# Three of the eleven down-projection units computed with seven block products in place of eight

## What is computed

```
def swiglu(x, w_gate, w_up, w_down):
    return (jax.nn.silu(x @ w_gate) * (x @ w_up)) @ w_down

h = h + 0.5 * swiglu(rms_norm(h, ln_ffn1[layer]), ffn1_w_gate[layer],
                     ffn1_w_up[layer], ffn1_w_down[layer])
```

## Time and profile before

| | us |
|---|---|
| median of 3 runs | 918.43 |
| the profiled execution, its own time | 919.42 |
| its span, first to last instruction | 917.6 |
| TensorE busy in the span | 905.8 (99%) |
| VectorE busy | 574.0 (63%) |
| ScalarE busy | 471.6 (51%) |
| share of the chain that ended last: TensorE / VectorE / DMA | 91% / 4% / 2% |

### The profile page before, as it was taken

One profiled execution on the slowest core, in us unless ns is written; L12 is line 12 of the kernel. 1 busy time (PEld: TensorE's weight loads), 2 busy tenths in 40 slices (PEclk: granted clock), 3 DMA queues, 4 the chain that ended last, 5 costly groups with the idle time before them and its releaser, 6 DMA issues.

```text
span 917.6 us, 11621 instructions
## 1 busy us (share of the span) xinstructions
PE 905.8 (99%) x4195; PEld 745.5 (81%) x4195; DVE 574.0 (63%) x724; ACT 471.6 (51%) x635; POOL 90.7 (10%) x170
## 2 busy tenths in 40 slices
PE   8999999999999999999999999999999999999997
PEld 7888888888888888888888888888876788888885
DVE  5656663574787766665467566644588776656542
ACT  6554443565685654444346445433478664444431
POOL 1100005623311100000002000000030000000000
PEclk9999999999999999999999999999999999999999
DMA  9898778558733888876557888874563388887611
GB/s 306 258 296 240 240 243 243 209 180 289 234 98 93 263 266 261 246 261 230 178 162 231 251 249 249 301 243 171 196 230 110 121 279 272 263 252 285 228 71 46
DMA packets 169758, 202.86 MB, mean 221 GB/s; under 512 B 15160, under 2 KB 139136, under 8 KB 169712
## 3 DMA queue, kind: packets, MB, share of 16 engines
q1 hardware_dynamic: 168752, 201.37, 67.5%
q0 software_dynamic: 512, 0.36, 0.4%
q10 hardware_dynamic: 448, 0.53, 0.2%
HBM read 184.39 MB, written 17.83 MB: 220 GB/s over the span
## 4 chain that ended last, share of the span: by engine, by line
PE 91%; DVE 4%; DMA 2%; issue 1%; ACT 1%; SPq 1%; POOL 0%; POOLq 0%; DVEq 0%; ACTq 0%
PE bank L535 58%; PE bank L574 18%; PE bank L580 9%; PE bank L596 2%; PE bank L764 1%; PE bank L639 1%; DVE w_lo L1767 1%; PE bank L795 1%; DMA raw<-in_ffn_w_up 1%; DMA x_bounce<-silu 0%; PE bank L817 0%; PE bank L741 0%; SPq L1055 0%; ACT junk L1399 0%; DVE hT_lo L1767 0%
## 5 line engine op out<-in xcount | busy, mean ns | idle before, releaser
L1767 DVE TENSOR_TENSOR w_lo<-raw,w_hi 128x2048 fp32r<-128x2048 f32 x149 | 340.2, 2292 | 185.5 <-ACT w_hi L1380 185.1
L1380 ACT ACTIVATE w_hi<-raw 128x2048 fp32r<-128x2048 f32 x154 | 294.4, 1916 | 194.3 <-PE bank L580 97.6
L535 PE MATMUL bank<-w_hi,xT_hi 128*128 128x512 f32 x816 | 318.8, 391 | 0.2 <-DVE w_lo L1774 0.2
L535 PE MATMUL bank<-w_lo,xT_hi 128*128 128x512 f32 x816 | 317.6, 389 | 0.0
L535 PE MATMUL bank<-w_hi,xT_lo 128*128 128x512 f32 x816 | 307.9, 389 | 0.0
L535 PEld LDWEIGHTS bank<-w_hi,xT_hi 128*128 128x128 f32 x816 | 153.2, 188 | 33.1 <-DVE w_lo L1774 0.6
L535 PEld LDWEIGHTS bank<-w_hi,xT_lo 128*128 128x128 f32 x816 | 153.2, 188 | 31.9
L535 PEld LDWEIGHTS bank<-w_lo,xT_hi 128*128 128x128 f32 x816 | 153.2, 188 | 31.3
L574 PE MATMUL bank<-w_hi,hT_hi 128*128 128x512 f32 x348 | 135.6, 390 | 0.0
L574 PE MATMUL bank<-w_lo,hT_hi 128*128 128x512 f32 x348 | 135.4, 389 | 0.0
L580 PE MATMUL bank<-w_hi,hT_lo 128*128 128x512 f32 x348 | 107.1, 389 | 0.0
(11 more groups left out here) (182 smaller groups left out, 599.7 us busy)
## 6 DMA issues: line engine op xcount, KB each, us to landing
raw<-in_ffn_w_down SPq DMA_DIRECT2D x88, 512.0 KB, 5.1
raw<-in_ffn_w_gate SPq DMA_DIRECT2D x86, 512.0 KB, 5.9
raw<-in_ffn_w_up SPq DMA_DIRECT2D x86, 512.0 KB, 7.0
raw<-in_a_w_qkv SPq DMA_DIRECT2D x24, 512.0 KB, 5.6
h_bounce<-silu SPq DMA_DIRECT2D x40, 256.0 KB, 7.0
xn<-h_bounce SPq DMA_DIRECT2D x160, 64.0 KB, 3.0
xn<-x_bounce SPq DMA_DIRECT2D x64, 64.0 KB, 2.0
raw<-in_a_w_o SPq DMA_DIRECT2D x8, 512.0 KB, 5.3
```

The lines of the kernel that those rows point to most:

```text
L535: mm = nc.tensor.matmul(bank[b][:, :], xs[:, kt, own(pos)], ws[:, slot(u), cols], start=(kt == 0 and i == 0), stop=(kt == KT - 1 and i == 2))
L1380: nc.scalar.activation(w_parts(u)[0], raw[:, slot(u), :], ACT.Copy).then_inc(s_hi, 1)
L1767: nc.vector.tensor_tensor(lo, raw[:, slot(u), :], hi.bitcast(F32), ALU.subtract).then_inc(s_lo, 1)
```

## The change

Three of the eleven down units (positions 2, 4 and 6 of the order, `SEVEN`) are computed with seven block products (21 matmuls in place of 24), by sums and differences of blocks:

- Four sums of h tiles for each such unit (`h_sum`, 128 x 128 each, and a copy `a1_copied` of the first rows' tiles), made in each loop turn of the gate and up part on VectorE, ahead of `mul(1, 0)` and the split of unit 4g+6. They are split too (`h_sums_high` on ScalarE, `h_sum_low` on VectorE) and held where `vec` was.
- Four sums of weight tiles: one in place in `raw` before the unit is split (`t_first`), three of 512 columns beside it (`t_sums`), split by `t_high` (ScalarE, 1536 columns) and `t_low` (VectorE). There is room for the three of one unit alone (over `xT_hi`, `xT_lo`); those of the next unit wait until TensorE has read them (`s_t_used`).
- Banks 4 to 7 gather four of the products over the three units; `seven_added` adds them into x with eight VectorE instructions after the last split.
- The order of the down part is two units of first rows, two of second rows, then unit by unit up to the seventh; the tiles of h are taken in the order `DN_ORDER`. The bias vectors are loaded later, since their place holds the sums until then.

The diff, cut to what computes and orders (new semaphores and views left out):

```
+DN_ORDER = [1, 3, 0, 5, 2, 6, 4, 7, 8, 9, 10]
+SEVEN = [2, 4, 6]
+N_SEVEN = len(SEVEN)
+SEVEN_END = SEVEN[-1] + 1
...
+        with nc.sbuf_tensor("t_raw", [P, KT * SEQ], F32) as t_raw:
+            pass
         xT_lo = sb("xT_lo", [P, KT, SEQ], F32R)
...
-        vec = sb("vec", [P, VEC_RING, D])
+        with nc.sbuf_tensor("vec", [P, VEC_RING, D], F32) as vec:
+            pass
+        h_sums = sb("h_sums", [P, VEC_RING, 2, BANK], F32R)
...
+            def three(b, lhs, rhs, start=False, stop=False):
+                (l_hi, l_lo), (r_hi, r_lo) = lhs, rhs
+                nc.tensor.matmul(bank[b][:, :], l_hi, r_hi, start=start, stop=False)
+                nc.tensor.matmul(bank[b][:, :], l_hi, r_lo, start=False, stop=False)
+                return nc.tensor.matmul(bank[b][:, :], l_lo, r_hi, start=False, stop=stop)
+            def seven(f, u, n):
...
+                T2, T4, T3 = range(3)
+                begin, end = n == 0, n == N_SEVEN - 1
+                pe.wait_ge(s_h_sums_lo, seven_no(f, n))
+                pe.wait_ge(s_t_lo, seven_no(f, n))
+                for b in (4, 5, 6, 7) if begin else ():
+                    take(b)
+                three(6, s_tile(3), t_tile(T3), begin, end)
+                three(5, s_tile(2), t_tile(T2), begin, end)
+                three(acc(1, 0), a_tile(1, 1), t_tile(T4)).then_inc(s_t_used, 1)
+                unit_ready(u)
+                three(7, s_tile(1), b_tile(0, 1), begin, end)
+                three(4, a_tile(0, 0), b_tile(0, 0), begin, end)
+                three(acc(0, 0), a_tile(0, 1), b_tile(1, 0))
+                three(acc(0, 1), s_tile(4), b_tile(1, 1)).then_inc(s_used, 1)
...
-                        rows_pass(u0 + GU_UNITS + i, 2 * i, FT, pos, hT_hi, hT_lo, ("down", f))
+                        rows_pass(u0 + GU_UNITS + i, 2 * DN_ORDER[i], FT, pos, hT_hi, hT_lo, ("down", f),
+                                  first=(i == 0))
                 pe.wait_ge(s_hT_lo[0], block_no(f, H_BLOCKS - 1))
-                down((0, 1, 2), 0)
+                down((0, 1), 0)
                 pe.wait_ge(s_hT_lo[1], block_no(f, H_BLOCKS - 2))
-                down((0, 1, 2), 1)
-                down((3, 4, 5, 6), 0)
-                down((3, 4, 5, 6), 1)
+                down((0, 1), 1)
+                for i in range(2, SEVEN_END):
+                    if i in SEVEN:
+                        seven(f, u0 + GU_UNITS + i, SEVEN.index(i))
+                    else:
+                        down((i,), 0)
+                        down((i,), 1)
...
+                        if i - UNITS_HELD in SEVEN:
+                            sp.wait_ge(s_t_sums, seven_no(f, SEVEN.index(i - UNITS_HELD)))
+                        load(u, [(dst[:, k, :], view[:, 2 * DN_ORDER[i] + k, :]) for k in range(2)])
...
-                for name in vectors:
-                    vector(name)
...
-                down(*range(8, DN_UNITS))
+                down(8, 9)
+                if "b_b_q" in vectors:
+                    vector("b_b_q", u0)
+                down(10)
+                for name in vectors:
+                    if name != "b_b_q":
+                        vector(name, u0)
...
-                if n == 2:
-                    sp.wait_ge(s_lamd, 1)
+                sp.wait_ge(s_used, u0 + GU_UNITS + SEVEN[n] + 1)
                 sp.dma_start(vec[:, n, :], src.to_broadcast([P, D])).then_inc(s_vec[n], 16)
...
+            def t_high(f, n):
+                act.wait_ge(s_t_sums, seven_no(f, n))
+                nc.scalar.activation(t_hi[:, 0:3 * BANK], t_raw[:, 0:3 * BANK], ACT.Copy).then_inc(s_t_hi, 1)
+            def h_sums_high(f, turn):
+                act.wait_ge(s_h_sums, turn + seven_no(f, 0))
+                nc.scalar.activation(h_sums[:, bass.ds(turn, 1), 0, :], vec[:, bass.ds(turn, 1), BANK:D],
+                                     ACT.Copy).then_inc(s_h_sums_hi, 1)
...
                     silu_gate(1, 0, g, turn)
+                    if turn is not None:
+                        h_sums_high(f, turn)
                     split(u0 + 4 * g + 6, turn)
...
-                split(u0 + 24)
+                split_with_t1(u0 + 24, f, 0)
+                silu_gate(1, 0, 5)
+                t_high(f, 0)
                 split(u0 + 25)
-                silu_gate(1, 0, 5)
-                split(u0 + 26)
+                split_with_t1(u0 + 26, f, 1)
                 h_hi(1, 4)
-                for i in range(27, 30):
-                    split(u0 + i)
+                split(u0 + 27)
+                t_high(f, 1)
+                split_with_t1(u0 + 28, f, 2)
                 h_last_hi(0)
                 h_last_hi(1)
+                split(u0 + 29)
+                t_high(f, 2)
                 for i in range(30, 33):
                     split(u0 + i)
+                act.wait_ge(s_used, u0 + GU_UNITS + SEVEN_END)
+                nc.scalar.activation(p1_copy, bank[4][:, :], ACT.Copy).then_inc(s_read[4], 1)
...
+            def t_first(f, u, n):
+                dve.wait_ge(s_raw[slot(u)], 32 * (u // UNITS_HELD + 1))
+                nc.vector.tensor_tensor(raw_tile(u, 0, 1), raw_tile(u, 0, 1), raw_tile(u, 0, 0),
+                                        ALU.add).then_inc(s_t1, 1)
+            def t_sums(f, u, n):
+                if n == 0:
+                    dve.wait_ge(s_used, u - SEVEN[0])
+                else:
+                    dve.wait_ge(s_t_used, seven_no(f, n) - 1)
+                dve.wait_ge(s_t1, seven_no(f, n))
+                t2, t4, t3 = [t_raw[:, BANK * i:BANK * (i + 1)] for i in range(3)]
+                link(nc.vector.tensor_tensor(t2, raw_tile(u, 0, 1), raw_tile(u, 1, 1), ALU.add))
+                nc.vector.tensor_tensor(t4, t2, raw_tile(u, 1, 0), ALU.add)
+                nc.vector.tensor_tensor(t3, t2, raw_tile(u, 0, 0), ALU.subtract).then_inc(s_t_sums, 1)
+            def t_low(f, n):
+                dve.wait_ge(s_t_hi, seven_no(f, n))
+                cols = slice(0, 3 * BANK)
+                nc.vector.tensor_tensor(t_lo[:, cols], t_raw[:, cols], t_hi[:, cols].bitcast(F32),
+                                        ALU.subtract).then_inc(s_t_lo, 1)
...
+                link(nc.vector.tensor_tensor(s_raw_tile(1), a_tile(1, 0), a_tile(1, 1), ALU.subtract))
+                link(nc.vector.tensor_tensor(s_raw_tile(2), a_tile(0, 0), s_raw_tile(1), ALU.subtract))
+                nc.vector.tensor_tensor(s_raw_tile(3), a_tile(1, 0), a_tile(0, 0), ALU.subtract)
+                nc.vector.tensor_tensor(s_raw_tile(4), a_tile(0, 1), s_raw_tile(2),
+                                        ALU.subtract).then_inc(s_h_sums, 1)
+            def a1_copied():
+                link(nc.vector.tensor_copy(a1_copy.rearrange("p (t q s) -> p t q s", t=2, q=4),
+                                           landed[0].rearrange("p (q t s) -> p t q s", q=4, t=4)[:, 0:2, :, :]))
...
+            def h_sum_low(f, turn):
+                dve.wait_ge(s_h_sums_hi, turn + seven_no(f, 0))
+                buf = bass.ds(turn, 1)
+                nc.vector.tensor_tensor(h_sums[:, buf, 1, :], vec[:, buf, BANK:D], h_sums[:, buf, 0, :].bitcast(F32),
+                                        ALU.subtract).then_inc(s_h_sums_lo, 1)
...
+                in_sbuf(dve, ("seven", f, 4))
+                nc.vector.tensor_tensor(p6_less, bank[5][:, :], p1_copy, ALU.subtract).then_inc(s_read[5], 1)
+                counted(into_x(0, 0, p1_copy, 0.5))
+                in_sbuf(dve, ("seven", f, 5))
+                nc.vector.tensor_tensor(p5_more, bank[7][:, :], p6_less, ALU.add).then_inc(s_read[7], 1)
+                counted(into_x(1, 0, p6_less, -0.5))
+                in_sbuf(dve, ("seven", f, 7))
+                counted(into_x(0, 1, p5_more, 0.5))
+                counted(into_x(1, 1, p5_more, 0.5))
+                dve.wait_ge(s_dve, t.last("dve"))
+                counted(into_x(1, 0, bank[6][:, :], -0.5))
+                ins = into_x(1, 1, bank[6][:, :], 0.5)
+                ins.then_inc(s_read[6], 1)
+                dve.wait_ge(s_dve, t.last("dve"))
+                in_sbuf(dve, ("seven", f, 6))
...
+                    if turn is not None:
+                        h_sum(f, turn)
                     if g == 0:
                         dve.wait_ge(s_rstd, rstd_count(name, 1))
                     mul(1, 0)
+                    if turn is not None:
+                        h_sum_low(f, turn)
...
                     mul(0, 0)
+                    if g < 4:
+                        a1_copied()
...
-                split(u0 + 24)
-                split(u0 + 25)
+                t_first(f, u0 + 24, 0)
                 h_last_turned(0)
                 dve.wait_ge(s_turned[1], block_no(f, H_BLOCKS - 1))
+                split(u0 + 24)
+                t_sums(f, u0 + 24, 0)
                 mul(1, 0, 5)
                 h_last_turned(1)
+                t_low(f, 0)
+                split(u0 + 25)
+                t_first(f, u0 + 26, 1)
                 split(u0 + 26)
                 h_lo(1, 4)
```

(11 more changed lines are left out.)

68 lines of the change are left out of this document (60 added, 8 removed).

## The result

The changed kernel takes 931.18 us (median of 4 runs, 930.35 to 931.89) against 919.0 us (4 runs, 918.35 to 919.94) before: ratio 1.0127, 95% interval 1.0115 to 1.0140. That is 12.2 us slower, outside the range forecast (911.5 to 929.5). The profiled execution took 930.35 us; its span is 928.5, 10.9 more than before.

The account below looks back on a forecast made before the run. TensorE, busy 99%, was taken to bound the kernel, so every wait put on it is paid. Removed matmuls -8.2, loop +7.4 and down part +5.6 gave +4.8 us: 923.2 us, range 911.5 to 929.5.

Parts of the forecast that it names:

- Removed, -8.2: Down units: 36 matmuls fewer at 0.2267 us each, all on the path, save 8.2 us.
- Loop, +7.4 forecast: Gate and up loop: sums delay ScalarE's copy and unit 4g+6's remainder; TensorE loses 0.62 us in each of 12 turns.
- late h at nothing: Loop: second-row h, sent some 3.4 us later, returns just before `h_lo` reads it; 0 us, up to 0.5 a turn.
- Down part, +5.6 forecast: Down part: second seven-product unit's weight sums come 1.29 us late, 1.4 with restart, in each of four feed-forwards.
- ruled it out: Down part, feed-forward 1: bank 2 is wanted at 422.6 and `mul` frees it at 421.3, so no wait.
- +4.8: Whole kernel: the sum -8.2 + 7.4 + 5.6 us, giving 923.2 against the median.
- rival 3: Loop: h returns later than `h_lo` wants it, 0.5 us more a turn, 6 in all: 929; chance 0.10 (or worse).
- The 7.1 us: Loop: time taken for h of the second rows to come back after it is sent.
- rival 1: Loop: sequencer steps hide behind short additions, TensorE waits about 0.1 a turn, 1.2 in all: 917.0; chance 0.19 with nearby.
- the rule: VectorE: next instruction starts when the pipe has emptied, semaphores cost nothing more; four additions take 1.16 us, time about 917.
- No wait at the first and third unit: Down part: first unit's sums ready before 428.03; third's end near 448.4, wanted at 449.8, 1.4 us of cover.
- `seven_added` covered: End of down part: eight VectorE additions end at 464.2, first rows at 465.5; 1.3 us of cover, priced at nothing.

Follow-up runs that it names:

- The removal alone: Kernel before with three matmuls left out in each of three down units (36 fewer), nothing added: 911.21 us.
- lighter loads: Changed kernel with half of each feed-forward weight load left out, except the first eight units of feed-forward 0: 924.6 us; same on the kernel before: 919.15.
- the doubled run: Changed kernel with the four h-sum additions of each loop turn made twice, ahead of `mul(1, 0)`: 948.1 us.

## Why the prediction was wrong

- **Removed, -8.2: right.** The removal alone gives 8.2, and with the added work well placed nothing of it is lost.
- **Loop, +7.4 forecast, +10.5 measured.** The quiet turn took 0.62, as forecast, and by the chain as written: from `h_lo` the four starts are 0.60, 0.43, 0.45 and 0.21 apart, against 0.60, 0.47, 0.47 and 0.21. That it fits to the hundredth is luck: the chain up to the end of the remainder was 0.09 shorter, and TensorE started 0.14 after it, where 0.05 was taken. The step that failed is the one that put late h at nothing: h "comes back just ahead of where `h_lo` of the next turn would read it, so I price it at nothing". For the blocks that the change sends later this held: in the second and third turns h was at most 0.04 late. But in the first loop turns of feed-forwards 1 and 3 `h_lo` reads the block of turn 0, which no sums stand ahead of and which the prediction didn't look at. It came 1.03 and 1.95 late, 3.0 us together, once the slack of 3.2 that had covered it was spent.
- **Down part, +5.6 forecast, +8.9 measured.** In feed-forwards 1 and 2 the second sums were late by the chain I wrote: 17.06 us after the start of the down part, forecast 16.99. The wait in full is 1.56, not 1.4: the chain ended 0.07 later, and TensorE starts 0.15 after the remainder, where 0.05 was taken. That is 0.6 in all. In feed-forwards 0 and 3 the block of h that stands ahead of `t_first` came back late, and the chain began later (ScalarE's copy of the third unit 1.48 and 0.71 us before TensorE's start in place of 2.44): 0.9 and 1.0 more. In feed-forward 3 `mul`, which frees bank 2, ended at 866.75, and TensorE wanted that bank 5.44 after its start, at 866.26: I take this for its wait at 866.85, 0.7 in full (the profile names no releaser; with lighter loads the wait is gone). I had ruled it out from feed-forward 1 alone.
- **Sum.** Late h is 3.0 + 1.9 + 0.7 = 5.6 of the 6.1 by which the profiled execution (+10.9) misses +4.8; lighter loads give 5.6 back between the profiled executions. This is rival 3, with its mechanism right and its place and size wrong. I gave it 0.10 and a price of 0.5 in every turn, having read a return that was in time as one that is always in time. The 7.1 us that I gave for h coming back is only the way out, up to SyncE's issue of the read. In the trace of before, the returns without cover were there to see (ScalarE's copy at 338.90, `h_lo` 0.46 idle at 774.44), and I read a feed-forward in which h was back with time to spare.
- **Cheap small steps, rival 1: half shown.** In this kernel's loop dependent additions are 0.43 to 0.45 apart, near the 0.47 taken; in the second set of the doubled run they are 0.32. What makes the difference was not tried. By the rule of the Trainium skill, "VectorE: DVE Perf Modes", "The DRAIN you can't avoid", four additions of 0.29 would take 1.16 us from first start to last end. The trace has 554.71 to 556.09, 1.38, so for the loop's own set the rows decide against it; for the second set, 594.14 to 595.28, it is 1.14, close to the rule. The prediction also gave the rule without its exception: the same page of the Trainium skill has a section, "Two Vector instructions with no wait between them", by which an instruction that nothing holds starts earlier, and the independent additions 0.20 apart with 0.28 of length agree.
- **No wait at the first and third unit, `seven_added` covered: right.** The eight additions of feed-forward 1 end at 469.28 and the residual begins at 471.03, 1.75 of cover (1.3 forecast).

## What to carry to other kernels

Work put ahead of an engine's critical step costs what the *waiting* engine loses: the same additions cost 11 us while ScalarE's copy of a unit stood behind them, and nothing once it stood ahead. Slack is cover for everything upstream, late transfers too; before spending it, look at the latest return of a transfer over all turns, those that the change leaves alone included, and not at a typical one. Where two engines hand a tile to and fro (`t_first`, copy, remainder), put an independent step between the hand-overs: one moved line was worth 8 to 10 us here.
